# First attention step moved into the last input-projection panels, with a new order of the key and query units and of the item exponentials, in a one-layer hybrid attention and GLA kernel

## What is computed

```python
h  = half_ffn(h, m_lat, 0, g_norm[l, 0], w_ffn_up[l, 0], w_ffn_down[l, 0])
p_lat = jnp.split(n_lat @ w_in[l], IN_SPLITS, axis=-1)     # q, k, v, GLA q k v z, decay, merge gates
q_lat = apply_rope(attn_heads(p_lat[0], ATTN_HEADS, g_q[l]), cos, sin)     # RMS norm per head, then rotary
k_lat = apply_rope(attn_heads(p_lat[1], ATTN_KV_HEADS, g_k[l]), cos, sin)
attn_lat = block_attention(q_lat, concat([k_lat, k_ctx]), concat([v_lat, v_ctx]))
gla_lat, _, _ = gla_bidirectional(p_lat, w_decay[l], b_decay[l], s_f, s_b)
h = h + m_lat[..., 5, :] * merge_branches(p_lat, attn_lat, gla_lat, ...)
h = half_ffn(h, m_lat, 2, g_norm[l, 2], w_ffn_up[l, 1], w_ffn_down[l, 1])
```

## Time and profile before

| what | value |
|---|---|
| median of 3 runs | 2821.98 us |
| the profiled execution, its own time | 2817.84 us |
| its span in the profile | 2816.0 us |
| TensorE busy | 2715.9 us, 96% |
| DVE, ACT, GpSimd busy | 53%, 22%, 19% |
| mean granted TensorE clock | 0.994 of 2.4 GHz |
| GLA items and group norms | about 1255 to 1472 us of the span |
| key, query and value units | about 1472 to 1595 us |
| end of the projection, start of attention | about 1601 us |

### The profile page before, as it was taken

How to read it: one execution, slowest core, us unless ns; L and a number is a source line. 1 busy time by engine, 2 the same in 40 slices (tenths; PEclk the granted TensorE clock), 3 DMA queues, 4 the chain that set the end, 5 groups by cost and what they waited for, 6 DMA issues and landing times.

```text
span 2816.0 us, 35086 instructions
## 1 busy us (share of the span) xinstructions
PE 2715.9 (96%) x14088; PEld 2214.6 (79%) x14088; DVE 1486.1 (53%) x2349; ACT 626.7 (22%) x1152; POOL 544.2 (19%) x468
## 2 busy tenths in 40 slices
PE   8999999999999999999999888999999999999998
PEld 3888888888888867876776677778778888888887
DVE  6644545344443473267555488867444444444444
ACT  4200000000000043243236478861120000000002
POOL 0065446455510000015320023230000000000001
PEclk9999999999999999999999999999999999999999
DMA  8121112232211121112233200014401111111111
GB/s 290 38 64 64 60 60 87 69 104 79 87 50 37 34 98 56 57 49 70 66 100 99 83 1 1 1 61 139 137 23 45 45 52 45 47 49 47 50 45 75
DMA packets 198289, 187.67 MB, mean 67 GB/s; under 512 B 7645, under 2 KB 149770, under 8 KB 198026
## 3 DMA queue, kind: packets, MB, share of 16 engines
q1 hardware_dynamic: 190160, 171.83, 19.2%
q10 hardware_dynamic: 7994, 13.97, 1.3%
HBM read 161.39 MB, written 24.38 MB: 66 GB/s over the span
## 4 chain that ended last, share of the span: by engine, by line
PE 84%; DVE 7%; ACT 5%; issue 3%; DMA 1%; ACTq 0%; POOL 0%; DVEq 0%; SPq 0%
PE psum L221 25%; PE psum L222 25%; PE psum L223 24%; DVE ptl L1970 2%; PE psum L1866 1%; ACT pth L1926 1%; PE psum L314 1%; ACT prob L1916 1%; PE psum L1497 1%; PE psum L1474 1%; PE psum L1883 1%; PE psum L1884 1%; DVE wl L198 1%; PE psum L408 1%; PE psum L570 0%
## 5 line engine op out<-in xcount | busy, mean ns | idle before, releaser
L221 PE MATMUL psum<-nh,wh 128*128 128x512 f32 (+2 forms) x1688 | 629.5, 373 | 1.4 <-DVE wl L198 1.4
L222 PE MATMUL psum<-nl,wh 128*128 128x512 f32 (+2 forms) x1688 | 615.0, 364 | 0.0
L223 PE MATMUL psum<-nh,wl 128*128 128x512 f32 (+2 forms) x1688 | 614.4, 364 | 0.0
L814 ACT ACTIVATE silu_a<-psum 128x512 f32<-128x512 f32 (+1 forms) x110 | 61.1, 556 | 1494.9 <-PE psum L223 1494.9
L196 DVE CAST wh<-raw 128x1024 fp32r<-128x1024 f32 (+1 forms) x173 | 123.7, 715 | 492.0 <-PE psum L223 491.9
L221 PEld LDWEIGHTS psum<-nh,wh 128*128 128x128 f32 (+1 forms) x1688 | 318.0, 188 | 66.3 <-issue 8.1
L222 PEld LDWEIGHTS psum<-nl,wh 128*128 128x128 f32 (+1 forms) x1688 | 317.8, 188 | 52.9 <-issue 4.4
L223 PEld LDWEIGHTS psum<-nh,wl 128*128 128x128 f32 (+1 forms) x1688 | 317.5, 188 | 52.6
L846 DVE SCALAR_TENSOR_TENSOR h<-psum,gates,h 128x512 f32<-128x512 f32 (+1 forms) x400 | 270.9, 695 | 155.3 <-PE psum L223 153.1
L221 PE MATMUL psum<-hidh,wh 128*128 128x512 f32 (+1 forms) x880 | 331.4, 377 | 11.6 <-DVE hidl L830 7.6
L222 PE MATMUL psum<-hidl,wh 128*128 128x512 f32 (+1 forms) x880 | 326.7, 371 | 0.0
(11 more groups left out here) (252 smaller groups left out, 3802.7 us busy)
## 6 DMA issues: line engine op xcount, KB each, us to landing
raw<-in_w_ffn_up_dram SPq DMA_DIRECT2D x88, 512.0 KB, 3.9
mod_part<-in_w_mod_dram SPq DMA_DIRECT2D x96, 256.0 KB, 4.2
raw<-in_w_ffn_down_dram SPq DMA_DIRECT2D x44, 512.0 KB, 3.6
raw<-in_w_in_dram SPq DMA_DIRECT2D x34, 512.0 KB, 3.8
mod_raw<-in_w_mod_dram SPq DMA_DIRECT2D x12, 1024.0 KB, 13.9
gates_saved<-staged ACTq DMA_DIRECT2D x40, 256.0 KB, 2.0
merge_gate<-gates_saved SPq DMA_DIRECT2D x8, 1024.0 KB, 5.0
x_rows<-in_x_dram SPq DMA_DIRECT2D x8, 512.0 KB, 8.4
```

The costliest lines, as they stand in the source:

```text
L221: pe.matmul(o, hi_w, hi_x, start=first, stop=False)
L222: pe.matmul(o, hi_w, lo_x, start=False, stop=False)
L223: return pe.matmul(o, lo_w, hi_x, start=False, stop=last)
L814: nc.scalar.activation(silu_a[:, c, 0:w], ps[c][:, 0:w], ACT.Silu).then_inc(self.a_free, 1)
```

## The change

1. The order of the 14 key, query and value units is now: 3 key units, 2 query units of heads 0 and 1, 3 value units, 6 query units. They start two slots earlier (118 instead of 120), the high copies stand at s + 5 and the low halves at s + 7, the sources are loaded along other panels, and both halves of the rotary table are loaded at once into two buffers.
2. ACT's exponentials for an item stand first among the GLA pieces of a slot, ahead of the squares, the group norm and the `qdec` exponentials, instead of last.
3. Step 0 of attention runs inside the projection: its scores on TensorE in slot 153, maxima and bias on DVE in slot 155, exponentials on ACT in slot 156, into a buffer of its own. The wait for the saved units stands ahead of step 2 on ACT instead of ahead of step 0.
4. PSUM banks are dealt out anew so that banks 0 and 1 are free for step 0: the projection's ring uses banks 2 and 3 instead of 1 and 2.

```diff
-    rope_t = at("rope_t", 136, [2, 512])
+    rope_t = [at("rope_t0", 136, [2, 512]), at("rope_t1", 168, [2, 512])]
...
+    prob_first = at("prob_first", 128, [TOK])
...
-    PAIR_BANKS = (4, 6, 7, 5, 0, 3)
-    RING_BANKS = (1, 2)
+    PAIR_BANKS = (4, 6, 7, 5, 0, 1)
+    RING_BANKS = (2, 3)
...
             if i == SRC_PANELS[0]:
                 gla_store(sp, N_GROUPS - 1)
-                rope_load(sp, 0)
-            if i == ROPE_PANEL:
-                rope_load(sp, 1)
+                rope_load(sp)
...
                     qk_pe(pe, h)
+                    first_pe(pe, h)
...
     def intra_act(act, h):
+        for n in range(N_ITEMS):
+            if ITEM_SLOTS[n] == h + 1 and n % N_SCORES:
+                act.wait_ge(g_lq, 4 * decayed(n) + 4)
+                for e in (eqs[n % 3], eks[n % 3]):
+                    nc.scalar.activation(e[:, :], e[:, :], ACT.Exp, scale=1.0 / GATE_NORM).then_inc(g_eq, 1)
         if h in OUT_SLOTS:
...
-        for n in range(N_ITEMS):
-            if ITEM_SLOTS[n] == h + 1 and n % N_SCORES:
...
-    QK_UNITS = []
-    for half_c in range(2):
-        QK_UNITS += [("k", 0, half_c)] + [("q", t, half_c) for t in range(4)] + [("v", 0, half_c)]
-    QK_UNITS += [("k", 0, 2), ("v", 0, 2)]
-    QK_SLOTS = [120 + 5 * x // 2 for x in range(len(QK_UNITS))]
-    SRC_PANELS = (28, 28, 28, 28, 30, 31, 31, 32, 33, 33, 34, 34, 34, 34)
-    ROPE_PANEL = 32
-    SS_BANKS, PERM_BANKS, V_BANK = (0, 3), (4, 5), 6
+    QK_UNITS = [("k", 0, c3) for c3 in range(3)] + [("q", 0, 0), ("q", 0, 1)] + [("v", 0, c3) for c3 in range(3)]
+    QK_UNITS += [("q", t3, c3) for t3 in range(1, 4) for c3 in range(2)]
+    QK_SLOTS = [118 + 5 * x // 2 for x in range(len(QK_UNITS))]
+    SRC_PANELS = (28, 28, 28, 28, 29, 30, 31, 31, 32, 32, 33, 33, 34, 34)
+    SS_BANKS, PERM_BANKS, V_BANK = (0, 1), (5, 7), 6
...
-            if h == QK_SLOTS[x] + 4:
+            if h == QK_SLOTS[x] + 5:
...
-            if h == QK_SLOTS[x] + 6:
+            if h == QK_SLOTS[x] + 7:
...
+    FIRST_SCORES, FIRST_MAXIMA, FIRST_EXP = 153, 155, 156
...
+    def first_pe(pe, h):
+        if h == FIRST_SCORES:
+            pe.wait_ge(k_lo, FIRST_LOWS)
+            pe.wait_ge(k_ln, len(normed_units))
+            att_score(pe, 0, False)
+            att_score(pe, 0, True)
...
-        score(0, False)
-        score(0, True)
+        pe.wait_ge(win_evac, N_UNITS)
+        pe.wait_ge(k_lo, N_K_LO)
+        pe.wait_ge(v_lo, 3)
         score(1, False)
         for i in range(N_STEP + 4):
+            if i == 1:
+                turn(0, (0, 1))
...
-            if 1 <= i <= N_STEP:
+            if 2 <= i <= N_STEP:
                 turn(i - 1, (0, 1))
...
+    def first_act(act, h):
+        if h == FIRST_EXP:
+            act.wait_ge(k_norm, len(normed_units))
+            exp_context(act, 0)
+            exp_latent(act, 0)
...
-        wait_saved(act, len(staged_units))
         for i in range(N_STEP + 4):
-            if i < N_STEP:
-                exp_context(i)
+            if i == 2:
+                wait_saved(act, len(staged_units))
+            if 1 <= i < N_STEP:
+                exp_context(act, i)
...
+    def first_dve(dve, h):
+        if h == FIRST_MAXIMA:
+            maxima(dve, 0)
+            bias(dve, 0)
```

More of the change, by code:

```diff
@@ L1200, in pieces @@
             qk_act(act, h)
+            first_act(act, h)
         for u, (i, c) in enumerate(win_units):
@@ L1528, in intra_act @@
                                      scale=1.0 / GATE_NORM).then_inc(g_qde, 1)
-        for n in range(N_ITEMS):
-            if ITEM_SLOTS[n] == h + 1 and n % N_SCORES:
-                act.wait_ge(g_lq, 4 * decayed(n) + 4)
-                for e in (eqs[n % 3], eks[n % 3]):
-                    nc.scalar.activation(e[:, :], e[:, :], ACT.Exp, scale=1.0 / GATE_NORM).then_inc(g_eq, 1)
     def intra_pool(pool):
@@ L1685, in src_load, with rope_load @@
         sp.dma_start(srcs[x % 4][:, 0:w], kvq_dram[n, :, t0:t0 + w]).then_inc(src_loaded[x % 4], 16)
[L1687 to L1691 removed]
+    def rope_load(sp):
+        for c, (t0, w) in enumerate(LAT):
+            sp.dma_start(rope_t[c][:, :, :], rope[:, :, t0:t0 + w].rearrange("a p t -> p a t")).then_inc(rope_loaded, 16)
     def qk_act(act, h):
@@ L1807, in qk_dve @@
                 nc.vector.tensor_tensor(src, src, sines[n % 2][:, :], ALU.add).then_inc(k_rot, 1)
+    FIRST_LOWS = sum(qk_copies[:4])
     N_K_LO = sum(qk_copies)
@@ L1831, in build, with prob @@
     context_scores = ps[4][:, 0:CTX]
+    def prob(i):
+        return probs[i % 3] if i else prob_first
     def turned_of(i, r):
@@ L1835, in turned_of, with att_score @@
         return ps[5 + (TG * i + r) % 2][:, 0:(b - a) * P]
+    FIRST_SCORES, FIRST_MAXIMA, FIRST_EXP = 153, 155, 156
+    def att_score(pe, i, context):
+        hd, qt = divmod(i, Q_BLOCKS)
+        kv = hd // (HEADS // KV_HEADS)
+        if context and i >= 1:
+            pe.wait_ge(exp_ctx, i)
+        if not context and i >= 2:
+            pe.wait_ge(exp_lat, i - 1)
+        for t0, w in ALL[2:] if context else LAT:
+            o = context_scores if context else latent_scores(i)[:, t0:t0 + w]
+            q = qs[:, hd, qt * P:(qt + 1) * P]
+            pe.matmul(o, q, kh[:, kv, t0:t0 + w], start=True, stop=False)
+            mm = pe.matmul(o, q, kl[:, kv, t0:t0 + w], start=False, stop=True)
+        mm.then_inc(s_ctx if context else s_lat, 1)
+    def first_pe(pe, h):
[4 more added lines that the diff above has]
+            att_score(pe, 0, True)
     EARLY_MERGE = (N_STEP - 1, N_STEP, N_STEP + 1, N_STEP + 3)
     def att_pe(pe):
-        pe.wait_ge(win_evac, N_UNITS)
-        pe.wait_ge(k_lo, N_K_LO)
-        pe.wait_ge(v_lo, 3)
         def score(i, context):
-            hd, qt = divmod(i, Q_BLOCKS)
-            kv = hd // (HEADS // KV_HEADS)
-            if context and i >= 1:
-                pe.wait_ge(exp_ctx, i)
-            if not context and i >= 2:
-                pe.wait_ge(exp_lat, i - 1)
-            for t0, w in ALL[2:] if context else LAT:
-                o = context_scores if context else latent_scores(i)[:, t0:t0 + w]
-                q = qs[:, hd, qt * P:(qt + 1) * P]
-                pe.matmul(o, q, kh[:, kv, t0:t0 + w], start=True, stop=False)
-                mm = pe.matmul(o, q, kl[:, kv, t0:t0 + w], start=False, stop=True)
-            mm.then_inc(s_ctx if context else s_lat, 1)
+            att_score(pe, i, context)
         def turn(i, groups):
@@ L1905, in att_pe, with exp_context, exp_latent @@
                 merge_early_pe(pe, merge_p0, EARLY_MERGE.index(i))
-    def att_act(act):
-        def exp_context(i):
-            act.wait_ge(nm_done, i + 1)
-            if i >= 3:
-                act.wait_ge(t_done, TG * (i - 2))
-            nc.scalar.activation(probs[i % 3][:, SEQ:TOK], context_scores, ACT.Exp, bias=nmax[:, i:i + 1],
-                                 scale=SCALE, accum_out=rs[:, i, 1:2]).then_inc(exp_ctx, 1)
-        def exp_latent(i):
-            nc.scalar.activation(probs[i % 3][:, 0:SEQ], latent_scores(i), ACT.Exp, bias=nmax[:, i:i + 1],
-                                 scale=SCALE, accum_out=rs[:, i, 0:1]).then_inc(exp_lat, 1)
+    def exp_context(act, i):
+        act.wait_ge(nm_done, i + 1)
+        if i >= 3:
+            act.wait_ge(t_done, TG * (i - 2))
+        nc.scalar.activation(prob(i)[:, SEQ:TOK], context_scores, ACT.Exp, bias=nmax[:, i:i + 1],
+                             scale=SCALE, accum_out=rs[:, i, 1:2]).then_inc(exp_ctx, 1)
+    def exp_latent(act, i):
+        nc.scalar.activation(prob(i)[:, 0:SEQ], latent_scores(i), ACT.Exp, bias=nmax[:, i:i + 1],
+                             scale=SCALE, accum_out=rs[:, i, 0:1]).then_inc(exp_lat, 1)
+    def first_act(act, h):
[3 more added lines that the diff above has]
+            exp_latent(act, 0)
+    def att_act(act):
         def high(i, groups):
@@ L1993, in att_dve @@
             before = 1 <= i <= N_STEP
-            if i < N_STEP:
-                maxima(i)
+            if 1 <= i < N_STEP:
+                maxima(dve, i)
             if before:
                 total(i - 1)
-            if i < N_STEP:
-                bias(i)
+            if 1 <= i < N_STEP:
+                bias(dve, i)
             if before:
```

48 lines of the change are left out of this document (22 added, 26 removed).

## The result

The changed kernel takes 2797.44 us, median of 5 runs (2790.16 to 2798.63), beside 2821.02 us for the kernel before, median of 5 runs on the same chip (2814.38 to 2822.41). The ratio is 0.9909, 95% interval 0.9895 to 0.9923: faster by 0.9%, 23.6 us by the medians (25.7 by the ratio, which is not the quotient of the medians), where 19.1 were forecast. The profiled execution took 2790.54 us with a span of 2788.7 us, 27.3 us under the span before.

The account below looks back on a forecast made before the run. TensorE holds 84% of the chain, so time is won only where it stands still. Gains of 10.9 + 2.8 + 5.4 = 19.1 us took the median of 2821.98 to a forecast of 2802 us, range 2795 to 2811.

Parts of the forecast that it names:

- Item exponentials ahead of the norm: ACT's item exponentials run before the group norm; TensorE's waits for item products shrink: 10.9 us gained, bounds 7.0 to 12.
- Key and query units: Copies one slot later: permutation waits of 6.4 us go, new waits of 3.6 us come; gain 2.8 us.
- (a): New TensorE wait at unit 0, starting at slot 118, whose source lands late: 0.7 to 0.9 us.
- (b): New TensorE wait at unit 2, where unit 0's four copies stand before ACT's square: 0.6 to 0.7 us.
- (c): The same wait at unit 3 with a full square: 1.7 us, plus 0.1 for a late evacuation.
- Entry: Start of attention: step 2's exponential at E + 8.4, not E + 14.8 (E: last projection matmul); net gain 5.4 us.
- The bound of 3.4 us: Lower end of the gain at attention's start, if TensorE's clock falls there for as long as before.
- (1): Rival: key units cost more, ACT's lateness reaching units 4 and 5; 2806 to 2809 us; chance 0.17 shared with (2).
- (2): Rival: attention's start bound by a later landing beside the 2 MB load, or low clock; about 2806 us; 0.17 with (1).
- (3): Rival: freed item waits return one item later, items give only 3 to 5 us; 2810 us; chance 0.09.
- (4): Rival: slower, SP's stops for sources delay panel loads, deciding from 20 us on; 2828 us or more; chance 0.03.
- (5): Rival: a wait such as `k_ln` holds TensorE in slot 153, costing about 2 us; 2804 us, within the forecast's 0.68.

Follow-up runs that it names:

- one_norm_back: The changed kernel with the exponentials of item 10 alone (slot 91) behind the first group norm again; 2797.6 us, 0.9919 of the kernel before.
- only_keys: The changed kernel with item exponentials last again and step 0 and its wait as before, leaving the new unit order and banks; 2812.1 us, 0.9973 of the kernel before.
- step0_out_late_wait: The changed kernel with step 0 of attention behind the projection, the wait for saved units still ahead of step 2; 2791.4 us, 0.9901 of the kernel before.
- only_late_wait: The kernel before with only ACT's wait for the saved units moved from ahead of step 0 to ahead of step 2; 2811.4 us, ratio 0.9977.
- norm_later: The changed kernel with DVE's group norm products seven slots behind the output instead of five, first three groups; 2796.7 us, 0.9921 of the kernel before.
- squares_first: The changed kernel with ACT's square of a key or query unit ahead of the copies in the same slot; 2790.6 us, 0.9904 of the kernel before.
- two_fixes: The changed kernel with SP's 2 MB load issued after the saved units land and squares ahead of copies; 2787.7 us, 0.9886 of the kernel before.
- two_fixes_step0_out: The changed kernel with the 2 MB load after the saved units' landing, squares before copies, step 0 behind the projection; 2791.2 us, 0.9898 of the kernel before.

## Why the prediction was right, point by point

The sign, the mechanism and the range (2795 to 2811 us) hold; 2797.4 was measured for 2802. The gain is 4.5 us larger than the sum by the medians. The sum left the clock out of the stages of the items and the keys. With the mean clock alike the runs gave 17.6 us for its 19.1; what they gave above it goes with a higher clock, which it did not foresee.

- **Item exponentials ahead of the norm: 10.9 us forecast.** TensorE's waits for items fell by 16.8 - 6.7 = 10.1 us. The three waits of 8.2 us are gone but for small rests (0.21 in the first group). What the step missed at this place: item 13's wait was taken as unchanged and grew from 2.5 to 3.4 us, since TensorE, no longer held up, comes earlier to a DVE that is late for its own reasons; one_norm_back shows it as 0.92 us. The stage gained 12.1 us and not 10.1 in the trace after, since no fall of the clock is in it; in six of eight traces the fall stands behind item 13 instead, and the gain is 10.0 to 10.6 us. Two bounds don't come out of their own figures: two delayed norms that hand on 1.1 us twice leave 6.5 us, not 7.0, and the whole of the 1.30 makes 11.2, not 12. The pairs that moved into a GpSimd subtraction cost no visible wait, as argued. That such a product is slowed by less than a whole subtraction was read too boldly, though: the product at 1362.50 began when only 0.55 us of this subtraction of the kernel before was left, so its 0.41 us can't tell a short block from a shared port.

```profile
1361.99 1.06 POOL L1557 TENSOR_TENSOR ek<-cum 128x256 f32<-128x256 f32 x1
```

- **Key and query units: 2.8 us forecast.** The permutation waits of 6.4 us went whole, the 0.2 kept for a norm behind a split did not come. Of the new waits the term (a) was mis-sized: unit 0 waits 0.17 us, not 0.9. (b) was 0.56 for 0.7 and (c) 1.62 for 1.8. So the new waits are 2.4 us, not 3.6, and 4.0 us are gained in waits. The stage gained 5.1 us with step 0's scores in it, 6.2 us without (only_keys): the rest is mostly a clock fall that went, 1.7 us behind the permutation wait of 3.0 us.
- **Entry: 5.4 us forecast, net.** To step 10 the entry is 7.1 us shorter in the trace after, and 5.8 to 6.7 in three kernels with the same entry; the scores inside cost 0.75 to 1.3 us. That leaves 4.5 to 6.3 us. Step 2's exponential stands at 8.3 us behind the last evacuation, where E + 8.4 was written; E lies a few tenths before the evacuation. The size is right. The heading was not: it credits "Step 0 inside the projection", while step0_out_late_wait and only_late_wait show that the late wait wins all of it, or all but a few tenths. The text had the reason in its own numbers: steps 0 and 1 "don't wait for the landing", and ACT would stand before the landing from E + 7 on. It did not ask what the late wait alone would give.
- **The clock as a lower bound.** The bound of 3.4 us supposed that a fall at the entry costs 2 us of TensorE's work. In the kernel before the fall ends at about 1617, while step 2's exponential starts at 1616.21, so its price has to be sought ahead of step 2; from step 2 to step 10 the kernel before and only_late_wait take 32.31 and 32.39 us. The clock of the kernel before, and the exponentials of steps 0 and 2 in only_late_wait, whose clock is full:

```profile
1610.00:1617.00 7.00, 6.32 (x22) 5.31 (x23) 3.96 (x11) 4.74 (x12) 0.00 (x0) 0.54 0.00 0
1617.00:1648.00 31.00, 27.78 (x194) 23.24 (x193) 27.15 (x65) 25.05 (x59) 3.69 (x6) 1.00 0.00 1
```

```profile
1600.04 0.47 ACT L1912 ACTIVATE prob<-psum,nmax 128x256 f32<-128x256 f32 x1 [3.13 <-DVE nmax L1963]
...
1604.89 0.47 ACT L1912 ACTIVATE prob<-psum,nmax 128x256 f32<-128x256 f32 x1
```

  From step 0's exponential to step 2's the kernel before takes 1616.21 - 1609.76 = 6.45 us, and four other kernels with a fall there 6.08 to 6.46 us; only_late_wait takes 4.85 and step0_out_late_wait 5.02 us at full clock. So a fall costs some 1.1 to 1.6 us (an estimate from these differences), not far under the 2 us supposed. Nor does the change rule it out. The trace after has 1.00 at the entry, but one_norm_back, norm_later and squares_first, with the same entry, have a fall behind their stops of 1.98, 2.37 and 1.91 us, in one_norm_back nearly to the 0.50 that the prediction excluded:

```profile
1592.00:1596.00 4.00, 2.73 (x12) 2.63 (x13) 2.48 (x7) 2.72 (x7) 0.00 (x0) 0.52 0.00 2
```

  The Trainium skill's rule (TensorE: Matmul & The Clock Gate, Part 1), by which small gaps might have lowered the clock at the entry, found no support in the trace after: 1.00 at the entry with 64% busy. The falls in the three other traces agree with it, but don't tell whether the small gaps or the one longer stop made them. Where the clock did cost, in the two stages before, I had not looked.
- **Sum.** Stages 24.3 us against 19.1: +1.2 us for the items, and 12.2 against 8.2 for keys and entry together. Of the 5.2 us missed in these two traces 3.4 are the two clock falls and 1.2 the waits at the sums; the item waits took 0.8 back, and the entry has the rest. The 1.7 us of the items stage are luck of this execution, as said.
- **Rivals.** (1) was refuted: the keys gained more than I counted, and nothing was handed on to units 4 and 5. (2): the landing does compete with the 2 MB load, as it did before, but at the time I had taken for it; the low clock did come in three kernels with this entry, for up to 1.3 us to step 10. (3) holds for a third of one wait. (4) did not come: SP's longest stop for a source is 11.3 us (`kl`), under the 20 us from which it would decide. (5) did not come: step 0's scores show no wait.

## What to carry to other kernels

A wait that guards an overlaid buffer belongs ahead of the first instruction that writes this buffer; one moved line was worth 6.5 us here, and the rebuilt step around it added nothing that the runs can tell. In an in-order queue put first what another engine waits for soonest, and ask of each wait removed who is late next: some of it comes back at the next late engine (0.92 of 2.84 us). When pricing a stop of TensorE, read the granted clock in the microseconds behind it too, and in several executions: a fall that is missing in one trace (193.64 us) stood in six of eight (195.15 to 195.73 us).

## What the runs showed of the hardware

The clock falls behind a stop in some executions and not in others with the same stop. Item 13's wait of 3.41 us (3.42 in two_fixes) is followed by full clock in two traces and by less in six. The changed kernel and two_fixes are one of each. The changed kernel:

```profile
1322.00:1332.00 10.00, 6.59 (x51) 5.04 (x50) 9.21 (x13) 2.28 (x5) 2.37 (x4) 1.00 0.49 157
```

two_fixes:

```profile
1322.00:1332.00 10.00, 6.58 (x33) 5.01 (x33) 9.78 (x14) 1.81 (x4) 2.66 (x3) 0.83 0.51 156
```

Falls stand behind short stops too. In two_fixes_step0_out a fall stands behind stops of 0.69, 1.33 and 0.59 us, and the longest fall of the stages looked at came behind stops of 2.08 and 1.28 us in norm_later, with 12 us and more at 0.50 while TensorE was busy without a gap. What decides between these cases stays open. I had not expected either that a 256 KB store would land in 7.7 us instead of 2.0 because a 2 MB load was issued 0.6 us earlier on another queue.
